# First pass of three projections: a tile's products moved from four turns behind to one, first weights in four parts, loads reordered

## The chip, the cores and the metric

The kernel runs on one core of a Trainium2 chip. The metric is the device time of one execution in microseconds (us); the kernel before takes 2210.08 us, the median of three runs (2209.09 to 2212.71). The profile comes from one more execution, of 2207.55 us, whose span of profiled work is 2205.8 us.

Names of engines: PE is TensorE with its matmuls, PEld its loading of the stationary operand, DVE is VectorE, ACT is ScalarE, POOL is GpSimd. SPq is the queue of SyncE, from which most DMAs are issued; ACTq are the DMAs that ScalarE issues.

## The reference

One inference step of a two-layer decoder, float32 throughout, for 1024 prompt rows and 32 sample rows that share the weights (D_MODEL is 1024):

```
layer 0: h0 = rmsnorm(x) @ even_w_in          # 1024 x 3584
         mix0 = dilated attention, retention  # of h0
         x1 = x + (mix0 * silu(gate columns of h0)) @ even_w_out    # 1024 x 1024
layer 1: h1 = rmsnorm(x1) @ odd_w_in          # 1024 x 2864
         mix1 = sparse attention              # of h1
         x2 = x1 + (mix1 * silu(gate columns of h1)) @ odd_w_out    # 1024 x 1024
         y = rmsnorm(x2)
```

The attention parts are not touched by the change. It concerns the three places where rows are multiplied with a weight matrix.

## The kernel before

The program is a row of phases, each with its own buffers and semaphores and a barrier of all engines at its end. In a phase every engine has its own list of instructions, in an order written out by hand, and each instruction starts when those ahead of it on its engine have started and the semaphores that it names have come. `project` is the first phase of work (h0). `project_out` is called twice: in the middle, for x1 and then, with no barrier between, h1 (called projection 2 here), and at the end of the program, for x2 and y (projection 3). `project` is projection 1. All three begin in the same way, and only this beginning, the first pass, is changed.

The rows are cut into nine tiles: eight of 128 prompt rows (t = 0 to 7) and one of the 32 sample rows (t = 8). The columns of the weights are cut into passes (seven of 512 columns in projection 1; three of 342, 342 and 340 in projection 3 and at the start of projection 2). In the first pass a tile goes through these steps:

- SPq loads it, 512 KB, into one of two buffers `x`. In projections 2 and 3 two gate loads of together another 512 KB go to a buffer `z` (line 680 and 683; in projection 2 both buffers lie in `cmp_w1`, which the trace shortens to `cmp_w`; in projection 3 the gate is one DMA). From t = 2 on the load waits until tile t - 2 has been turned.
- ACT takes the sum of squares and its root (L352, L355), or the SiLU of the gate (L806); DVE scales the rows (L419, L421) or multiplies them with the gate (L896).
- PE turns the tile: eight transposes by a product with the identity matrix into one of two PSUM buffers `tps` (L518, L1034).
- ACT copies it out rounded, as `y_hi` (L360, L827), and DVE writes what was lost by the rounding, `y_lo` (L427, L910).
- PE makes the 24 matmuls of a tile's product (L527, L1047): for each of 8 blocks k of 128 rows of the weights, y_lo with w_hi, y_hi with w_lo, y_hi with w_hi. DVE takes the product out of PSUM (`take_product`, L445, L939) and SPq stores it.

The weights of a pass are cut in the same way into `w_hi` (ACT, L366, L833) and `w_lo` (DVE, L436, L922), from one buffer `w_raw` that one DMA fills: 2048 KB in projection 1, 1368 KB in the others. Weights of the passes lie in turns in two halves of w_hi and w_lo.

The constant LAG = 4 sets the order on PE: tiles 0 to 4 are turned, then PE waits for the whole of the first weights (`w_cut`), then come the product of tile 0, the turn of tile 5, the product of tile 1, and so on. WEIGHT_AT = 2 puts the cutting of the first weights on ACT and DVE behind their work on tile 2. Their load is issued by ACT once the rows of tile 0 have landed. The loads of the weights of the second pass, of the gain `g` (first in projection 1) and of the two first pieces of `w_side` (weights for the sample rows) stand behind the loads of all nine tiles on SPq, and the stores of the first pass behind those.

Ahead of projection 1 is a phase of its own in which SPq loads the identity matrix (`constants_shared`, 64 KB) and waits for it.

```
543                for t, n in tiles:
544                    turn(t, n)
545                    if t == LAG:
546                        pe.wait_ge(w_cut, 1)
547                    if t >= LAG:
548                        pe.wait_ge(yT_written[(t - LAG) % 2], (t - LAG) // 2 + 1)
549                        products(0, t - LAG)
```

## Time and profile before

| | |
|---|---|
| median of three runs | 2210.08 us (2209.09 to 2212.71) |
| the profiled execution | 2207.55 us |
| its span | 2205.8 us, 34764 instructions |
| PE busy | 1964.5 us (89%) |
| DVE, ACT, POOL busy | 849.7, 703.7, 508.4 us |
| DMA | 261.54 MB, mean 119 GB/s |

Each row of a timeline gives the start in us, how long it took, the engine, the line of the kernel, the operation with output and input, how many were merged, and in brackets how long the engine had been idle before it and what ended that. A busy PE is the sum of its matmuls' times; they overlap, and their distance is less than their length. The idle PE of the program's first 40 us, and of the same stage of the two other projections, is what the following reads.

### The profile page before, as it was taken

What the parts mean: (1) busy time and instruction counts of PE and PEld (TensorE: products, weight loads), DVE (VectorE), ACT (ScalarE), POOL (GpSimd) and SP (SyncE); (2) the same over time, 40 slices, a digit from 0 to 9 for tenths busy, and PEclk for the clock granted to TensorE, in tenths of its full rate; (3) what the DMA queues carried; (4) which work ended last, traced back from release to release, by engine and by line L of the source; (5) the groups of instructions that cost most, each with busy time, mean ns of one, the idle gap of its engine ahead of it and who ended that gap; (6) DMA issues with size and microseconds to landing.
All of it is one profiled execution on the core that took longest, in us unless ns stands there. A gap on an engine that the chain in (4) does not pass through costs nothing. (4 is left out here: it accounts for less than half of the span.)

```text
span 2205.8 us, 34764 instructions
## 1 busy us (share of the span) xinstructions
PE 1964.5 (89%) x13406; PEld 1444.6 (65%) x13406; DVE 849.7 (39%) x2373; ACT 703.7 (32%) x1555; POOL 508.4 (23%) x621
## 2 busy tenths in 40 slices
PE   4999998997883998999969999994999999999596
PEld 4777775565661987788855555553666666666495
DVE  4212212564442334122312112123666666666433
ACT  4100001553322222010012232323656666566312
POOL 0000000876640000000031211101454444445000
PEclk9999999999995999999989999997999999999798
DMA  3444434545595753744182323106000000000565
GB/s 131 175 142 142 141 131 124 176 118 152 163 242 165 239 189 108 241 154 147 48 242 96 135 74 135 49 1 162 7 21 21 16 21 21 6 11 11 194 214 182
DMA packets 163025, 261.54 MB, mean 119 GB/s; under 512 B 33746, under 2 KB 113296, under 8 KB 158512
## 3 DMA queue, kind: packets, MB, share of 16 engines
q1 hardware_dynamic: 141712, 207.83, 29.7%
q0 software_dynamic: 4608, 33.56, 4.2%
q10 hardware_dynamic: 16544, 17.95, 2.9%
q8 instruction: 109, 1.79, 0.3%
q14 instruction: 52, 0.43, 0.1%
HBM read 210.57 MB, written 55.77 MB: 121 GB/s over the span
## 5 line engine op out<-in xcount | busy, mean ns | idle before, releaser
L1573 POOL TENSOR_SCALAR sparse_pr<-sparse_pr,sparse_coef,sparse_gate 128x63 f32<-128x63 f32 (+8 forms) x384 | 247.4, 663 | 324.6 <-DVE sparse_coef L1537 324.6
L1047 PE MATMUL x_acc<-x_w_hi,x_y_lo 128*128 128x478 f32 (+3 forms) x768 | 274.7, 358 | 0.0
L1047 PE MATMUL x_acc<-x_w_lo,x_y_hi 128*128 128x478 f32 (+3 forms) x768 | 269.5, 351 | 0.0
L1047 PE MATMUL x_acc<-x_w_hi,x_y_hi 128*128 128x478 f32 (+3 forms) x768 | 269.1, 350 | 0.0
L2606 PE MATMUL ss_ps_h<-ss_xT,cmp_w 128*128 128x508 f32 x512 | 244.0, 594 | 0.8 <-ACT ss_xT L2445 0.8
L1475 ACT ACTIVATE sparse_pr<-sparse_pr,sparse_nmax 128x63 f32<-128x63 f32 (+8 forms) x384 | 227.8, 599 | 3.9 <-DVE sparse_nmax L1530 3.9
L1575 POOL TENSOR_SCALAR dilated_pr<-dilated_pr,dilated_coef 128x1024 f32<-128x1024 f32 (+7 forms) x64 | 109.5, 1725 | 408.1 <-DVE dilated_coef L1537 408.1
L1404 PE MATMUL sparse_ps_t<-constants_shared,sparse_pr 128*128 128x128 f32 (+1 forms) x1184 | 170.2, 281 | 11.3 <-ACT sparse_prT L1298 6.3
L527 PE MATMUL h_acc<-h_w_hi,h_y_lo 128*128 128x512 f32 x448 | 177.6, 397 | 0.0
L1530 DVE CUSTOM_DVE_ANT_0 sparse_pr<-sparse_ps_s,constants_sparse 128x63 f32<-128x63 f32 (+4 forms) x384 | 144.5, 421 | 85.4 <-PE sparse_ps_s L1392 85.3
L527 PE MATMUL h_acc<-h_w_hi,h_y_hi 128*128 128x512 f32 x448 | 175.2, 391 | 0.0
L527 PE MATMUL h_acc<-h_w_lo,h_y_hi 128*128 128x512 f32 x448 | 175.1, 391 | 0.0
L1404 PEld LDWEIGHTS sparse_ps_t<-constants_shared,sparse_pr 128*128 128x128 f32 (+1 forms) x1184 | 126.0, 140 | 74.5 <-issue 50.5
L1047 PEld LDWEIGHTS x_acc<-x_w_hi,x_y_lo 128*128 128x128 f32 x768 | 146.4, 191 | 25.1 <-issue 14.7
L1392 PE MATMUL sparse_ps_s<-sparse_kT_all,sparse_qT 64*128 64x512 f32 (+3 forms) x800 | 154.5, 484 | 2.7 <-ACT sparse_kT_all L1298 1.3
L1047 PEld LDWEIGHTS x_acc<-x_w_lo,x_y_hi 128*128 128x128 f32 x768 | 146.4, 191 | 10.2
L1047 PEld LDWEIGHTS x_acc<-x_w_hi,x_y_hi 128*128 128x128 f32 x768 | 146.0, 190 | 10.8
L1431 PE MATMUL sparse_ps_o<-sparse_prT,sparse_v_all 128*64 128x128 f32 x2112 | 148.9, 280 | 0.0
L1298 ACT COPY sparse_prT<-sparse_ps_t 128x512 f32<-128x512 f32 (+3 forms) x176 | 90.3, 513 | 175.7 <-PE sparse_ps_t L1404 175.5
L445 DVE COPY h_out<-h_acc 128x512 f32<-128x512 f32 x56 | 38.7, 692 | 248.9 <-PE h_acc L527 244.4
L1431 PEld LDWEIGHTS sparse_ps_o<-sparse_prT,sparse_v_all 128*64 128x64 f32 x2112 | 112.2, 136 | 25.7 <-issue 25.7
L2606 PEld LDWEIGHTS ss_ps_h<-ss_xT,cmp_w 128*128 128x128 f32 x512 | 86.1, 190 | 54.9 <-issue 53.6
(345 smaller groups left out, 2761.8 us busy)
## 6 DMA issues: line engine op xcount, KB each, us to landing
h_w_side<-in_even_w_in SPq DMA_DIRECT2D x16, 896.0 KB, 5.0
h<-h_out SPq DMA_DIRECT2D x56, 256.0 KB, 2.0
h_w_raw<-in_even_w_in SPq DMA_DIRECT2D x6, 2048.0 KB, 8.0
x_w_side<-in_odd_w_in SPq DMA_DIRECT2D x16, 716.0 KB, 4.8
x_w_raw<-in_odd_w_in SPq DMA_DIRECT2D x5, 1912.0 KB, 8.7
h<-x_out SPq DMA_DIRECT2D x40, 239.0 KB, 2.2
ev_unit<-in_cache_a_k SPq DMA_DIRECT2D x4, 2048.0 KB, 9.6
ev_unit<-in_cache_a_v SPq DMA_DIRECT2D x4, 2048.0 KB, 11.1
```

Of the source, the lines that this page charges most:

```text
L445: nc.vector.tensor_copy(outb[:, b, 0:width(i)], acc[b][:, 0:width(i)]).then_inc(evacuated[b], 1)
L527: last = nc.tensor.matmul(acc[b][:, 0:width(i)], rows[:, k, t * P:(t + 1) * P], buffer_of(cols, i)[:, k, :], start=(k == 0 and a == 0), st ...
L1047: last = nc.tensor.matmul(acc[b][:, 0:passes[p][3]], left[:, k, t * P:(t + 1) * P], weights(right, p)[:, k, :], start=(k == 0 and a == 0), ...
L1298: ins = nc.scalar.copy(to, src) if scale is None else nc.scalar.activation(to, src, ACT.Copy, scale=scale)
L1392: ins = nc.tensor.matmul(ps_s[c % 2][e][:, a - c0:b - c0], qT[i % 2][half, t * P:(t + 1) * P], rhs, start=True, stop=True)
L1404: last = nc.tensor.transpose(to[0:w, c - c0:c - c0 + P], pr[u % UB][:, e, c:c + w], con("ident"))
L1431: ins = nc.tensor.matmul(out, lhs, rhs, start=k == first and x == 0 and c == a, stop=k == end - 1 and last_one)
L1475: nc.scalar.activation(row, row, ACT.Exp, scale=-1.0, bias=nmax[u % UB][:, e * NBR + br:e * NBR + br + 1], accum_out=lsum[u % UB][:, e * N ...
L1530: nc.vector.tensor_tensor_reduce(out=pr[u % UB][:, e, a:b], in0=ps_s[c % 2][e][:, a - c0:b - c0], in1=bias, scale=1.0, scalar=so_far, op0= ...
L1573: nc.gpsimd.tensor_scalar(row, row, one, gate[:, t, 2 * i + e, (br + 1) % 3:(br + 1) % 3 + 1], ALU.mult, ALU.mult).then_inc(scaled, 1)
L1575: nc.gpsimd.tensor_scalar(row, row, one, None, ALU.mult).then_inc(scaled, 1)
L2606: ins = nc.tensor.matmul(ps_h[c][:, 0:4 * NCS], comp.w1[m][:, l, c * P:(c + 1) * P], xT[m][:, :, l % KD, s:s + NCS], start=l == 0, stop=l ...
```

## The change

In all three projections:

- PE: tile 0 and tile 1 are turned, then comes the product of tile 0, then the turn of tile 2, the product of tile 1, and so on: the product of tile t follows the turn of tile t + 1. LAG and WEIGHT_AT are gone.
- The first weights are loaded, rounded and cut in four parts of two blocks k each, with a semaphore for each load and one that counts the parts that are cut (`first_cut`). PE waits for part k // 2 at blocks k = 0, 2, 4, 6 of the first product.
- SPq issues: rows of tile 0 (in projection 1 then the identity and `g`), weight part 0, rows of tile 1, parts 1 to 3, rows of tile 2. From there on each tile's load is followed by a store of the product three tiles back, and the load of the second pass's weights stands behind the rows of tile 4. `g` (projections 2 and 3) and `w_side` come behind the rows of the last tile.
- ACT and DVE: parts 0 and 1 are cut around their work on tile 1, parts 2 and 3 behind the copy of tile 0. DVE takes the product of tile t - 2 in its step on tile t. The second pass's weights are rounded on ACT in its step on tile 6, and cut on DVE behind the product of tile 5, in its step on tile 7. The residual of tile t is loaded by ACT in its step on tile t.

In projection 1 alone: the phase for the identity matrix is gone, and its load is one of the phase; the mean with its epsilon, made by a small DVE instruction (L417) between the square and the root, is now the scale and bias of the root. Branches of `project` that no call used are deleted.

```diff
-LAG = 4
-WEIGHT_AT = 2
+FIRST_PARTS = 4
@@ project, SPq
-                for t, n in tiles:
...
-                for i in range(n_chunks):
-                    if i + 1 < n_chunks:
-                        sp.wait_ge(w_cut, i + 1)
-                        load_w(sp, i + 1)
-                    if i == 0:
-                        for s in range(WS):
-                            load_side(s)
+                load_rows(0, P)
+                constants.load(sp, ident_in)
+                sp.dma_start(g[:, :], gain.partition_broadcast(P)).then_inc(gain_in, 16)
+                load_first(0)
+                load_rows(1, P)
+                for j in range(1, FIRST_PARTS):
+                    load_first(j)
+                for t, n in tiles[2:]:
+                    load_rows(t, n)
+                    if t == 4:
+                        load_w(1)
+                    if t >= 3:
+                        store(0, t - 3)
+                for s in range(WS):
+                    load_side(s)
+                for t in range(NT - 2, NT):
+                    store(0, t)
@@ project, ACT
-                act.wait_ge(loaded[0], 16 * n_loads)
-                load_w(act, 0)
+                act.wait_ge(eps_ready, 1)
+                stats(0, P)
+                first_high_part(0)
+                stats(1, P)
+                first_high_part(1)
+                evacuate(0)
+                for j in range(2, FIRST_PARTS):
+                    first_high_part(j)
+                for t, n in tiles[2:]:
                     stats(t, n)
-                    if t:
-                        evacuate(t - 1)
-                    if t == WEIGHT_AT:
-                        w_high_part(0)
+                    evacuate(t - 1)
+                    if t == CUT_AFTER + 1:
                         w_high_part(1)
@@ project, DVE (project_out alike)
+                rows_of(0, P)
+                first_low_part(0)
+                rows_of(1, P)
+                first_low_part(1)
+                y_low_part(0)
+                for j in range(2, FIRST_PARTS):
+                    first_low_part(j)
+                for t, n in tiles[2:]:
                     rows_of(t, n)
-                    if t:
-                        y_low_part(t - 1)
-                    if t == WEIGHT_AT:
-                        w_low_part(0)
-                    if t > LAG:
-                        take_product(0, t - LAG - 1)
+                    y_low_part(t - 1)
+                    take_product(0, t - 2)
+                    if t - 2 == CUT_AFTER:
+                        w_low_part(1)
@@ project, PE (project_out alike)
                     for k in range(KD):
+                        if i == 0 and t == 0 and k % KP == 0:
+                            pe.wait_ge(first_cut, k // KP + 1)
...
+                turn(0, P)
+                for t, n in tiles[1:]:
                     turn(t, n)
-                    if t == LAG:
-                        pe.wait_ge(w_cut, 1)
-                    if t >= LAG:
-                        pe.wait_ge(yT_written[(t - LAG) % 2], (t - LAG) // 2 + 1)
-                        products(0, t - LAG)
+                    pe.wait_ge(yT_written[(t - 1) % 2], (t - 1) // 2 + 1)
+                    products(0, t - 1)
@@ project_out, SPq
+                load_gated(0, P)
+                load_first(sp, 0)
+                load_gated(1, P)
+                for j in range(1, FIRST_PARTS):
+                    load_first(sp, j)
+                for t, n in tiles[2:]:
                     load_gated(t, n)
+                    if t == 4:
+                        load_w(sp, 1)
+                    if t >= 3:
+                        store(0, t - 3)
@@ build
-        with Phase(nc) as phase, nc.Block() as block:
-            constants_in = phase.semaphore("constants_in")
...
```

Three places of the instruction order show it. The first is the start of SPq's list, in projection 1. Before:

```order
L2922 DMA constants_shared<-in_const 128x128
L159 ISA
L284 UNCONDITIONAL_BRANCH
L287 DMA h0_g<-in_even_norm 128x1024
L296 DMA h0_x<-in_x_prompt 128x1024 x8
L296 DMA h0_x<-in_x_sample 32x1024
L281 DMA h0_w_raw<-in_even_w_in 128x8x512
```

and now:

```order
L250 DMA h0_x<-in_x_prompt 128x1024
L2858 DMA constants_shared<-in_const 128x128
L282 DMA h0_g<-in_even_norm 128x1024
L254 DMA h0_w_raw<-in_even_w_in 128x2x512
L250 DMA h0_x<-in_x_prompt 128x1024
L254 DMA h0_w_raw<-in_even_w_in 128x2x512 x3
L250 DMA h0_x<-in_x_prompt 128x1024 x2
L272 DMA h0<-h0_out 128x512
L250 DMA h0_x<-in_x_prompt 128x1024
L261 DMA h0_w_raw<-in_even_w_in 128x8x512
L272 DMA h0<-h0_out 128x512
L250 DMA h0_x<-in_x_prompt 128x1024
```

What moved: the rows of tile 0 go first and the weights stand second, fourth and fifth instead of on ACT behind the landing of tile 0 (where they were `h0_w_raw`, 128x8x512); a store of `h0_out` and the second pass's weights (128x8x512) stand between loads of rows.

The second is the start of PE's list, in projection 1, with the waits. tps0 and tps1 hold turned tiles, acc0 a product. Before:

```order
L518 MATMUL h0_tps0<-constants_shared,h0_x 128x128 [waits h0_rows_ready0]
L518 MATMUL h0_tps0<-constants_shared,h0_x 128x128 x7
L518 MATMUL h0_tps1<-constants_shared,h0_x 128x128 [waits h0_rows_ready1]
L518 MATMUL h0_tps1<-constants_shared,h0_x 128x128 x7
L518 MATMUL h0_tps0<-constants_shared,h0_x 128x128 [waits h0_yT_written0,h0_rows_ready0]
L518 MATMUL h0_tps0<-constants_shared,h0_x 128x128 x7
L518 MATMUL h0_tps1<-constants_shared,h0_x 128x128 [waits h0_yT_written1,h0_rows_ready1]
L518 MATMUL h0_tps1<-constants_shared,h0_x 128x128 x7
L518 MATMUL h0_tps0<-constants_shared,h0_x 128x128 [waits h0_yT_written0,h0_rows_ready0]
L518 MATMUL h0_tps0<-constants_shared,h0_x 128x128 x7
L527 MATMUL h0_acc0<-h0_w_hi,h0_y_lo 128x512 [waits h0_yT_written0,h0_w_cut]
L527 MATMUL h0_acc0<-h0_w_lo,h0_y_hi 128x512
```

and now:

```order
L431 MATMUL h0_tps0<-constants_shared,h0_x 128x128 [waits h0_rows_ready0,h0_ident_in]
L431 MATMUL h0_tps0<-constants_shared,h0_x 128x128 x7
L431 MATMUL h0_tps1<-constants_shared,h0_x 128x128 [waits h0_rows_ready1]
L431 MATMUL h0_tps1<-constants_shared,h0_x 128x128 x7
L442 MATMUL h0_acc0<-h0_w_hi,h0_y_lo 128x512 [waits h0_first_cut,h0_yT_written0]
L442 MATMUL h0_acc0<-h0_w_lo,h0_y_hi 128x512
...
L442 MATMUL h0_acc0<-h0_w_hi,h0_y_lo 128x512 [waits h0_first_cut]
...
L431 MATMUL h0_tps0<-constants_shared,h0_x 128x128 [waits h0_yT_written0,h0_rows_ready0]
L431 MATMUL h0_tps0<-constants_shared,h0_x 128x128 x7
L442 MATMUL h0_acc1<-h0_w_hi,h0_y_lo 128x512 [waits h0_yT_written1]
```

What moved: the first product comes after two turns instead of five, and it waits for `first_cut`, part by part, instead of for `w_cut`; each later tile's turn stands between two products.

The third is DVE's list in projection 2: `cmp_w1_1` is the gating of a tile's rows, `x1_y_lo` the cutting of a turned tile, `x1_w_lo` that of weights, `x1_out` the taking of a product. Before:

```order
L896 TENSOR_TENSOR cmp_w1_1<-cmp_w1_1 128x1024 x2
L910 TENSOR_TENSOR x1_y_lo<-x1_tps0,x1_y_hi 128x8x128
L896 TENSOR_TENSOR cmp_w1_1<-cmp_w1_1 128x1024
L910 TENSOR_TENSOR x1_y_lo<-x1_tps1,x1_y_hi 128x8x128
L922 TENSOR_TENSOR x1_w_lo<-x1_w_raw,x1_w_hi 128x8x342
L896 TENSOR_TENSOR cmp_w1_1<-cmp_w1_1 128x1024
L910 TENSOR_TENSOR x1_y_lo<-x1_tps0,x1_y_hi 128x8x128
L896 TENSOR_TENSOR cmp_w1_1<-cmp_w1_1 128x1024
L910 TENSOR_TENSOR x1_y_lo<-x1_tps1,x1_y_hi 128x8x128
L896 TENSOR_TENSOR cmp_w1_1<-cmp_w1_1 128x1024
L910 TENSOR_TENSOR x1_y_lo<-x1_tps0,x1_y_hi 128x8x128
L939 TENSOR_TENSOR x1_out<-x1_acc0,x1_res 128x342
```

and now:

```order
L828 TENSOR_TENSOR cmp_w1_1<-cmp_w1_1 128x1024
L854 TENSOR_TENSOR x1_w_lo<-x1_w_raw,x1_w_hi 128x2x342
L828 TENSOR_TENSOR cmp_w1_1<-cmp_w1_1 128x1024
L854 TENSOR_TENSOR x1_w_lo<-x1_w_raw,x1_w_hi 128x2x342
L842 TENSOR_TENSOR x1_y_lo<-x1_tps0,x1_y_hi 128x8x128
L854 TENSOR_TENSOR x1_w_lo<-x1_w_raw,x1_w_hi 128x2x342 x2
L828 TENSOR_TENSOR cmp_w1_1<-cmp_w1_1 128x1024
L842 TENSOR_TENSOR x1_y_lo<-x1_tps1,x1_y_hi 128x8x128
L876 TENSOR_TENSOR x1_out<-x1_acc0,x1_res 128x342
L828 TENSOR_TENSOR cmp_w1_1<-cmp_w1_1 128x1024
L842 TENSOR_TENSOR x1_y_lo<-x1_tps0,x1_y_hi 128x8x128
L876 TENSOR_TENSOR x1_out<-x1_acc1,x1_res 128x342
```

What moved: the cut of tile t - 1 stands behind the gating of tile t as before, but the product of tile t - 1 now needs it at once, where there were three tiles of turned rows in stock.

## Rows read from the trace of the kernel before

**Rows 1.** Waits of PE, one query for each projection's stage: total us, times, longest

```profile
PE h_tps L518 <- DVE h_x L421: 28.0, 4, 15.0
...
PE x_tps L1034 <- DVE cmp_w L896: 37.7, 5, 25.5
...
PE x_tps L1034 <- DVE x_x L896: 24.9, 4, 13.4
```

**Rows 2.** Timeline of the program's start, projection 1

```profile
0.73 0.38 SPq L2922 DMA_DIRECT2D constants_shared<-in_const  x1
...
9.50 1.28 ACT L352 ACT_TABLE_LOAD   x1 [9.50 <-DMA h_x<-in_x_prompt]
...
13.70 1.28 DVE L421 SCALAR_TENSOR_TENSOR h_x<-h_x,h_stat,h_g 128x1024 f32<-128x1024 f32 x1
...
15.04 3.79 PE L518 MATMUL h_tps<-constants_shared,h_x 128*128 128x128 f32 x16 [15.04 <-DVE h_x L421]
...
22.84 3.61 ACT L366 CAST h_w_hi<-h_w_raw 128x4096 fp32r<-128x4096 f32 x1
...
26.49 4.43 DVE L436 TENSOR_TENSOR h_w_lo<-h_w_raw,h_w_hi 128x4096 fp32r<-128x4096 f32 x1 [1.78 <-ACT h_w_hi L366]
```

**Rows 3.** Timeline of PE in projection 1: turns and first matmul

```profile
35.73 1.97 PE L518 MATMUL h_tps<-constants_shared,h_x 128*128 128x128 f32 x8 [0.98 <-DVE h_x L421]
...
37.35 0.78 PE L527 MATMUL h_acc<-h_w_hi,h_y_lo 128*128 128x512 f32 x1
...
44.92 1.04 PE L518 MATMUL h_tps<-constants_shared,h_x 128*128 128x128 f32 x8
...
51.26 1.04 PE L518 MATMUL h_tps<-constants_shared,h_x 128*128 128x128 f32 x8
```

**Rows 4.** Timeline of projection 2's first pass

```profile
695.66 2.36 DVE L896 TENSOR_TENSOR cmp_w<-cmp_w 128x1024 f32<-128x1024 f32 x2 [7.99 <-ACT cmp_w L806]
...
696.94 3.64 PE L1034 MATMUL x_tps<-constants_shared,cmp_w 128*128 128x128 f32 x16 [25.53 <-DVE cmp_w L896]
...
698.94 0.32 SPq L680 DMA_DIRECT2D cmp_w<-mix  x1
...
699.99 1.23 DVE L910 TENSOR_TENSOR x_y_lo<-x_tps,x_y_hi 128x1024 fp32r<-128x1024 f32 x1 [1.97 <-ACT x_y_hi L827]
...
704.34 1.06 ACT L806 ACTIVATE cmp_w<-cmp_w 128x1024 f32<-128x1024 f32 x1 [4.38 <-DMA cmp_w<-h]
...
717.22 0.63 PE L1047 MATMUL x_acc<-x_w_hi,x_y_lo 128*128 128x342 f32 x1
...
722.96 1.09 PE L1034 MATMUL x_tps<-constants_shared,cmp_w 128*128 128x128 f32 x8
...
724.08 0.32 SPq L680 DMA_DIRECT2D cmp_w<-mix  x1
...
727.63 1.03 PE L1034 MATMUL x_tps<-constants_shared,cmp_w 128*128 128x128 f32 x8
...
731.11 1.06 ACT L806 ACTIVATE cmp_w<-cmp_w 128x1024 f32<-128x1024 f32 x1 [5.92 <-DMA cmp_w<-h]
...
733.49 1.09 PE L1034 MATMUL x_tps<-constants_shared,cmp_w 128*128 128x128 f32 x8 [1.07 <-DVE cmp_w L896]
```

**Rows 5.** Stretches of projection 2: start:end and length, busy us by engine, PEclk, DMA share, GB/s

```profile
701.00:703.00 2.00, 0.00 (x0) 0.00 (x0) 0.22 (x1) 0.00 (x0) 0.00 (x0) 1.00 0.98 346
...
705.00:707.00 2.00, 0.29 (x2) 0.29 (x3) 1.57 (x2) 2.00 (x3) 0.00 (x0) 0.50 0.44 167
```

**Rows 6.** DMA issues of projection 1's stage: size, median us to landing

```profile
h_x<-in_x_prompt SPq DMA_DIRECT2D x8, 512.0 KB, 3.8
...
h_w_raw<-in_even_w_in ACTq DMA_DIRECT2D x1, 2048.0 KB, 7.8
```

**Rows 7.** Timeline of PE in projection 3: first turn, first matmul

```profile
2062.69 3.43 PE L1034 MATMUL x_tps<-constants_shared,x_x 128*128 128x128 f32 x16 [13.43 <-DVE x_x L896]
...
2083.15 0.64 PE L1047 MATMUL x_acc<-x_w_hi,x_y_lo 128*128 128x342 f32 x1
```

More of the change, by code:

```diff
@@ L395, in _ @@
-                if residual is not None:
-                    load_side_residual(0)
-                for i in range(1, n_chunks):
-                    for t in range(NT):
-                        if residual is not None:
-                            load_residual(i, t)
-                        if t == CUT_AFTER and i + 1 < n_chunks:
-                            w_high_part(i + 1)
+                    nc.scalar.copy(weights(w_hi, i), w_raw[:, :, 0:width(i)]).then_inc(w_high, 1)
+                act.wait_ge(eps_ready, 1)
```

337 lines of the change are left out of this document (123 added, 214 removed).

## The prediction

> **What bounds the kernel now.** The page gives PE 1964.5 us of the 2205.8 us span, so what a stage is worth is PE's idle time in it. I read the waits of PE first. In the three stages PE waits almost only to turn rows: 28.0 us in projection 1, 37.7 in projection 2 (25.5 of it ahead of the first turn), 24.9 in projection 3 (13.4 ahead of the first turn) [rows 1]. Then the timelines, to see what those waits end in. In projection 1 the first turn is at 15.04 and the first product at 37.35 [rows 2, 3]; in projection 2 they are at 696.94 and 717.22, in projection 3 at 2062.69 and 2083.15 [rows 4, 7]. These 20 to 22 us hold five turns and nothing else for PE; from the first product on it hardly stops (one more wait of 1.07 us in projection 2 [rows 4]). So the term to work out is when the first product can start, and what comes back later in the pass.
>
> **Projection 1, the start.** The identity load at 0.73 and its phase go; the rows of tile 0 are issued at that time instead. A 512 KB load of rows takes a median 3.8 us to land [rows 6]: 4.6. Before, ACT began at 9.50 and DVE could scale at 13.70 [rows 2], 4.2 us for table loads, square and root; the small DVE step that leaves lay beside the second table load, so I count nothing for it. Scaling is at 8.8, and 1.3 later, at 10.1, PE turns tile 0 at the low clock, 2.0 us (35.73 shows one at that pace [rows 3]), to 12.1. ACT rounds part 0 (a quarter of 3.61, 0.9), takes tile 1's root, rounds part 1: done by 12. Then its copy of tile 0, 1.0, ends at 13.1. DVE: part 0 (a quarter of 4.43, 1.1) to 11.2, tile 1's scaling 1.5 to 12.7, part 1 to 13.8, y_lo of tile 0 (1.2) to 15.0. I add 0.3, since tile 1's rows are behind `g` and part 0 in the queue. **The first product starts at 15.3, not 37.35: 22.0 us earlier.** Parts 2 and 3 are cut at 16.1 and 17.2; the product reaches them after 12 and 18 of its 24 matmuls, 2.7 and 4.0 us on at the high clock. The cover of part 3 is thus 2 us; 3.7 MB are ahead of its landing, which at the 300 to 350 GB/s of a loaded stretch [rows 5] is 11 to 12 us, at about 14.
>
> What comes back: turns 2, 3 and 4 now stand between products, at about 1.04 each [rows 3]: -3.1. Tile 0's product took 44.92 - 37.35 = 7.57 us, a later tile with its turn 51.26 - 44.92 = 6.34, the product alone then 5.4 [rows 3]: the low clock cost 2.1. Now PE is busy from 10.1 almost without a gap, and I count half of this back, +1.0. At the pass's end DVE cuts the second weights (4.43) between the product of tile 5 and the scaling of tile 8; the scaling is then 6.8 us behind the start of turn 7, and PE wants it at 6.4: with y_lo of tile 7 behind it -0.7. Row loads have slack: 6.4 us per tile for 512 KB. **Sum: 22.0 - 3.1 + 1.0 - 0.7 = 19.2 us.**
>
> **Projection 2, the start.** Up to the first turn at 696.94 nothing changes. ACT: SiLU of tile 0, done when the gating starts at 695.66 [rows 4], part 0 (342 of 512 columns, so 0.6), SiLU of tile 1 when its rows are in. Ahead of these now lie 2.45 MB instead of 2.1; at about 340 GB/s that is 1.1 us more, 696.7. Then part 1, and the copy of tile 0 behind its turn at 698.9, to 699.95. DVE: gating of tile 1 to 699.0, part 1 (0.75) to 699.8, y_lo 699.95 to 701.2. First product: **701.3, not 717.22: 15.9 us earlier.** From the turns to the product no gap is left. After those two turns the granted clock went to 1.00 (2.4 GHz) at 701, with PE idle, and was back at 0.50 (1.2 GHz) at 705 [rows 5]; the new product begins inside that stretch, so the low clock's price in the first product (722.96 - 717.22 = 5.74 against 4.67 - 1.0 = 3.7 [rows 4], less what is idle: 1.7) comes back. Turns 2 to 4: -3.1. The idle 1.1 before goes into the new sum of stalls.
>
> The stalls are the dear unknown. A tile's rows are 1 MB, its load waits for the turn two tiles back, and behind its landing come SiLU 1.06, gating 1.23, turn 1.0 [rows 4]. Landing took from 698.94 to 704.34, 5.4 us, beside the weights, and at worst from 724.08 to 731.11, 7.0 us [rows 4]. PE needs 4.67 per tile [rows 4], so two tiles give 9.3 us; less the last three items 6.0 are left for a load. Worked through: turn 2 can start at 706.6, while product 0 ends at 705.05 (-1.5, and 0.25 for y_lo of tile 1). Loads 3 and 4 fit. The second weights, 1368 KB or 4.1 us of the queue at 340 GB/s, are ahead of load 5, which lands near 720.8: -2.2. Loads 6 and 7 fit. The cut of the second weights (4.43 x 342/512 = 3.0) ahead of gating tile 8: -0.5. Together 4.5. Bounds: 0 each if every load lands in under 6.0, 9 to 10 if all land in 7.0 (two tiles then take 10.3, 0.5 more per tile or 3.5 in all), the second weights cost their 4.1 in full and turn 2 its 1.5; I take 4.5, nearer the 5.4 row. **Sum: 15.9 - 3.1 + 1.7 + 1.1 - 4.5 = 11.1 us.**
>
> **Projection 3** is the same chain with the first turn at 2062.69: first product at 2067.1 instead of 2083.15 [rows 7], 16.0. Turns -3.1, the clock +1.4 (it was low for 3.0 us), no wait of before to give back, stalls -4.5: **9.9 us** (16.0 - 3.1 + 1.4 - 4.5 = 9.8, rounded up for one gate DMA less).
>
> **Costed at nothing:** earlier stores and later `g` and `w_side` (wanted only in the second pass, some 13 us behind their issue; if that cover goes, 1 or 2 us); SPq's wait for a product's copy ahead of the next load (this ends about when the turn does that the load waits for anyway); the dead branches.
>
> Total 19.2 + 11.1 + 9.9 = 40.2 us, of 2207.55 in the profiled execution. That one lies 2.5 us under the median of the runs, so from 2210.08: **2169.9, I say 2170 us**. No part behind the three passes is shared with them; what PE gains there nothing else holds up.
>
> **A rule against the change.** The trace has 512 KB in 3.8 us and 2048 KB in 7.8 [rows 6]: if parts of 512 KB each took their 3.8 in turn, the last would land 7.4 us later. But rows, gain and weights in one queue overlap, and the stage reaches 346 GB/s [rows 5], so I take the queue as one stream. The Trainium skill (DMA: Bandwidth & Descriptors, Bandwidth) says to batch DMAs to at least 1 MiB for 75% of peak. The trace agrees for one DMA alone, not for a queue of them; by that rule this is rival A.
>
> **Rivals.**
> - A, late loads: the parts and the rows land one after another. For it: the 7.0 us landing, and a DMA share of 0.98 in projection 2 [rows 4, 5]. Against: PE hardly waited in the old pass, at the same pace of loads. Part 3 would come 7.4 us later with a cover of 2 and 1, so 4 to 5 us in projection 1, and the full stalls (10 instead of 4.5) in the two others: 40 - 5 - 11 = 24, so 2186 us.
> - B, less stall: every load lands in under 6.0 and the clock is up from the first matmul on. 1 + 3.5 + 3.5 more: 2162 us.
> - C, slower than before: the clock. With row loads gating every tile, PE may stand between products long enough for the clock to fall, and then stay at 1.2 GHz for the pass. For it: PE is at 0.50 at 705 in projection 2, where it waits 37.7 - 25.5 = 12.2 us in four turns [rows 1, 5]. Against: turns behind the wait of 1.07 still take 1.09, the high clock [rows 4]. A turn takes 1.97 at the low clock and 1.04 at the high one [rows 3]; a product at the same ratio 7.0 instead of 3.7. That is 4.2 more per tile, 34 per projection: 2210 - 40 + 68 = 2238 us. It decides for slower from about 10 low tiles of 16 on, where 40 / 4.2 is reached, and needs waits of several us at every tile. The Trainium skill (TensorE: Matmul & The Clock Gate, Loop structure matters more than you think) names a DMA wait ahead of the matmuls as what makes them run at the low clock; here no wait that long is expected.
> - D, no gain: the early start only moves the wait, to the start of the second pass, if its weights are cut no earlier than before (DVE has them at about 736 in my chain, the pass begins at 743). It would need 7 us and more of delay in all three: 2208 us.
>
> **Chances.** Forecast 0.65 (its own range 2163 to 2178), A 0.19, B 0.08, C 0.05, D 0.03. A difference under about 0.2%, 4.4 us, can't be told from none here. Faster 0.92, same 0.03, slower 0.05. The range, 2158 to 2188, takes in B and A with their bounds and leaves out C and D.
>
> **What the new profile would show.** First matmul of the products near 15.3, about 4.4 us behind the first turn in projections 2 and 3, with the high clock within the first product. PE waits in the first pass of about 1, 4 and 4 us, the longest ahead of turn 5 for the loads behind the second weights. Second passes 19, 11 and 10 us nearer to their first turns or the start. Wrong would be: a first product that waits at block 4 or 6 for `first_cut`, waits ahead of every turn, or a product of 7 us in the middle of a pass of projection 2 or 3.

## The result, and the profile after

The changed kernel takes **2175.76 us** (median of 4 runs, 2174.89 to 2176.33) against 2209.59 us beside it (2206.5 to 2212.71): ratio 0.9846, 95% interval 0.9831 to 0.9861, so 33.8 us less. A second session gave 2176.61 against 2208.36, ratio 0.9857 (0.9842 to 0.9872). The forecast was 2170, range 2158 to 2188: the time is inside it, and the gain smaller than forecast. The profiled execution took 2175.72 us, span 2173.9, so 31.9 of the forecast's 40.2 us are seen in the spans.

The waits of PE after, by stage (total us, times, longest); they answer to [rows 1]:

```profile
PE h_tps L431 <- DVE h_x L361: 10.9, 3, 10.1
PE h_acc L442 <- DVE h_y_lo L367: 0.8, 2, 0.5
...
PE x_tps L973 <- DVE cmp_w L828: 29.4, 3, 23.7
PE x_tps L973 <- DVE cmp_w L835: 3.2, 1, 3.2
PE x_acc L988 <- DVE x_y_lo L842: 0.5, 1, 0.5
...
PE x_tps L973 <- DVE x_x L828: 17.9, 3, 13.4
```

Projection 1 has lost all waits but the one ahead of its first turn and 1.6 us in four small ones. Projections 2 and 3 keep that too, and two more: 2.6 and 2.0 us ahead of turn 1, and 3.2 and 2.5 us ahead of turn 5. (Line 828 is the gating. Line 835 is another operation, the scaling of x1's rows for h1; its wait, ahead of a turn at 777.78, lies behind the first pass.)

Projection 1's start after, from the timeline (start, duration, instruction, [idle before it <- releaser]), to be laid beside [rows 2, 3]:

```profile
4.29 1.28 ACT L319 ACT_TABLE_LOAD   x1 [4.29 <-DMA h_x<-in_x_prompt]
...
8.65 1.28 DVE L361 SCALAR_TENSOR_TENSOR h_x<-h_x,h_stat,h_g 128x1024 f32<-128x1024 f32 x1
...
10.08 1.94 PE L431 MATMUL h_tps<-constants_shared,h_x 128*128 128x128 f32 x8 [10.08 <-DVE h_x L361]
...
14.92 0.79 PE L442 MATMUL h_acc<-h_w_hi,h_y_lo 128*128 128x512 f32 x1 [0.30 <-DVE h_y_lo L367]
...
22.22 1.04 PE L431 MATMUL h_tps<-constants_shared,h_x 128*128 128x128 f32 x8
```

The chain runs as worked out: table load, scaling at 8.65 (8.8 was forecast), turn at 10.08 (10.1), first product at 14.92 (15.3; 37.35 before).

Projection 2's first pass after, to be laid beside [rows 4]:

```profile
670.71 1.28 ACT L732 ACT_TABLE_LOAD   x1 [32.73 <-PEq L159]
...
678.83 1.97 PE L973 MATMUL x_tps<-constants_shared,cmp_w 128*128 128x128 f32 x8 [23.70 <-DVE cmp_w L828]
680.98 1.06 ACT L732 ACTIVATE cmp_w<-cmp_w 128x1024 f32<-128x1024 f32 x1 [1.90 <-DMA cmp_w<-h]
683.35 1.97 PE L973 MATMUL x_tps<-constants_shared,cmp_w 128*128 128x128 f32 x8 [2.55 <-DVE cmp_w L828]
685.26 0.65 PE L988 MATMUL x_acc<-x_w_hi,x_y_lo 128*128 128x342 f32 x1
...
692.73 0.43 SPq L585 DMA_DIRECT2D x_w_raw<-in_even_w_out  x1
...
695.89 0.54 SPq L597 DMA_DIRECT2D cmp_w<-mix  x1
...
705.65 1.06 ACT L732 ACTIVATE cmp_w<-cmp_w 128x1024 f32<-128x1024 f32 x1 [6.37 <-DMA cmp_w<-h]
...
708.01 1.94 PE L973 MATMUL x_tps<-constants_shared,cmp_w 128*128 128x128 f32 x8 [3.17 <-DVE cmp_w L828]
...
714.31 0.93 PE L973 MATMUL x_tps<-constants_shared,cmp_w 128*128 128x128 f32 x7
```

The second weights (1368 KB) are issued at 692.73, tile 5's rows behind them at 695.89. They are there only when SiLU starts at 705.65, and PE has waited 3.17 us. Then comes what no step of the forecast had: turn 5 takes 1.94 us, the pace of the low clock, where turns 2 to 4 take 1.04 to 1.09. The next turn follows after 6.3 us, not 4.6. (A turn's distance to the next is taken from start to start.)

For this and the other kernels I use three durations from each profile: P1, from the start of the span to VectorE's taking of tile 7's product in projection 1's first pass; P2 and P3, from VectorE's first instruction in projections 2 and 3 to the same point there. The last columns are the median and its ratio to the kernel before in the same session. Names are explained with the experiments.

```
                    P1     P2     P3    median   ratio (95% interval)
before            86.78  67.13  64.71  2209.59
before, again     85.66  66.83  64.81  (one run, 2206.85)
after             67.54  58.17  57.37  2175.76  0.9846 (0.9831-0.9861)
after, again      66.69  58.27  58.22  2176.61  0.9857 (0.9842-0.9872)
p1_only           66.44  66.63  66.15  2190.02  0.9910 (0.9896-0.9924)
one_part          75.11  63.01  63.15  2191.68  0.9915 (0.9901-0.9929)
lag2              98.38  82.38  76.22  2246.99  1.0156 (1.0137-1.0176)
late_w            66.42  56.32  54.81  2173.31  0.9840 (0.9826-0.9854)
warm              66.05  57.70  57.88  2174.31  0.9842 (0.9825-0.9859)
quick             67.42  56.22  55.34  2167.88  0.9816 (0.9802-0.9829)
quick_late        68.86  55.00  57.79  2170.47  0.9837 (0.9820-0.9854)
quick_warm        65.91  55.41  52.37  2168.80  0.9799 (0.9785-0.9812)
spread            67.72  55.47  52.34  2165.22  0.9786 (0.9773-0.9799)
spread_warm       65.94  52.48  50.56  2163.55  0.9783 (0.9770-0.9797)
```

### The profile page after: what moved, and what is told of

Its sections match the earlier page's. It is cut to its first block and busy times, and to the rows that moved or that the text cites. A ratio compares the mean times of both kernels' runs of the same rounds, so it can differ in the third digit from the quotient of the medians.

```text
span 2173.9 us, 34766 instructions
## 1 busy us (share of the span) xinstructions
PE 1963.1 (90%) x13406; PEld 1442.1 (66%) x13406; DVE 848.3 (39%) x2374; ACT 704.9 (32%) x1564; POOL 506.3 (23%) x621
## 5 line engine op out<-in xcount | busy, mean ns | idle before, releaser
L988 PEld LDWEIGHTS x_acc<-x_w_hi,x_y_lo 128*128 128x128 f32 x768 | 146.7, 191 | 27.4 <-issue 14.6
```

The source lines that it names most:

```text
L988: last = nc.tensor.matmul(acc[b][:, 0:passes[p][3]], left[:, k, t * P:(t + 1) * P], weights(right, p)[:, k, :], start=(k == 0 and a == 0), ...
```

## Experiments

### Are the three projections independent, and is the rest of the program touched?

**before_again** is the kernel before and **after_again** the changed one, both unedited. **p1_only** has the changed `project` and the `project_out` of before.

> The kernel before, profiled a second time. Between the end of projection 1's first pass and the start of projection 2 the five profiles with the new projection 1 lost 2.1 to 3.0 us against the one profile of before. Theory A (scatter: that one profile, at 2207.55 against a median of 2209.3, was quick there): here the stretch from the last product of projection 1 to projection 2's first instruction takes 323 to 325 us instead of 321.6. Theory B (a cost of the change in code that it doesn't touch): 321.6 within 0.5.

> The kernel after the change, timed in the same session as the two below. 2173 to 2177. The two waits of about 3 us ahead of turn 5 in projections 2 and 3 stand there again, with the low clock behind them, if they are properties of the program: 2.5 to 3.5 us and 2.0 to 3.0 us. That the first product of projection 1 starts at 15.2 and the pass ends 19 to 20.5 us earlier than before's repeats too.

> Projection 1 as after the change, projections 2 and 3 as before it. Theory (each projection pays for itself, nothing behind it is shared): the 19.2 us that the profile after shows at the last product of projection 1 stay, so the median stands 16 to 19 us below before's, 2191 to 2194. Rival (the two later projections pay only because they start in another state of queues and clock, or the first one's gain is eaten behind it): a gain under 14 us. It also tells whether the 3.0 us lost between projection 1 and projection 2 belong to the change: if they do, projection 2's first load stands 16.2 us earlier than before's here too; if they are scatter between executions, somewhere between 16 and 20.

Measured: p1_only is 19.3 us below before, just outside the 16 to 19 expected; its P2 is before's within 0.5 us and its P3 1.4 longer. The rival (under 14) falls. From projection 1's last product to projection 2's first instruction the profile of before took 321.6 us, before_again 323.6, after 324.6, after_again 323.8 and p1_only 324.1; over all profiles taken it is 321.4 to 324.8, with nothing in common among the short ones. So this is scatter, and before's profiled execution was at the quick end. From projection 2's tile 7 to projection 3 it is 1299.0 to 1302.4 us, and here scatter may not be all: the three profiles with the `project_out` of before have 1299.0 to 1299.7, ten of the eleven with the new one 1300.2 to 1302.4 (the last is quick, 1299.3). Some 1.5 us of the gain may be lost there; the rows do not say by what, and no run tested it. The three passes alone gain 34.8 us by the means of both pairs of profiles (19.1, 8.8 and 7.0). The spans show 31.9 and 32.0, the medians 33.8 and 31.8.

The wait ahead of turn 5 repeats, 3.34 and 3.10 us, and so does the low clock behind it (expected were 2.5 to 3.5 and 2.0 to 3.0, so the second is just above). Projections 2 and 3 after, again, from the timeline of PE:

```profile
706.56 1.76 PE L973 MATMUL x_tps<-constants_shared,cmp_w 128*128 128x128 f32 x7 [3.34 <-DVE cmp_w L828]
...
2065.00 1.33 PE L973 MATMUL x_tps<-constants_shared,x_x 128*128 128x128 f32 x5 [3.10 <-DVE x_x L828]
```

(The rows end within the turns: 7 turns of 1.76 and 5 of 1.33 are 0.25 us each, against 0.13 at the high clock.)

### What are the four parts worth?

```diff
-FIRST_PARTS = 4
+FIRST_PARTS = 1
-load_first(0); load rows of tile 1; load_first(1 to 3)
+load rows of tile 1; load_first(0)
-first_high_part(0); tile 1; first_high_part(1); evacuate(0); ...
+tile 1; evacuate(0); first_high_part(0)      (VectorE likewise)
```

> After's order of turns and products, but the first weights as one load of 2048 KB behind tile 1's rows, cut in one piece (hi about 3 us on ScalarE, lo about 3.4 us on VectorE) behind tile 0's evacuation. Theory A (the parts matter where products begin with the weights, and the passes are paced by PE once they have begun): the first product begins 7 to 8 us later in projection 1 and 5 to 7 us later in projections 2 and 3; of that the stall ahead of turn 5 gives back 2 to 3 us in each of the latter, so the sum is 11 to 17 us slower than the full change, 2187 to 2193. Theory B (rows, not weights, limit: the passes are bound by their loads): projection 1 loses its 7 but projections 2 and 3 end where they do now, 2181 to 2184. If the parts were worth nothing and the order alone paid, 2176.

Measured: 2191.68, theory A's range. P1 is 7.6 to 8.4 us longer than in the two profiles after, P2 4.8, P3 4.9 to 5.8: 18 in all, 16 in the medians. The price is one row in each projection, the wait for the whole cut; here projection 2, timeline of PE:

```profile
688.95 1.97 PE L957 MATMUL x_tps<-constants_shared,cmp_w 128*128 128x128 f32 x8 [1.24 <-DVE cmp_w L815]
695.95 0.62 PE L972 MATMUL x_acc<-x_w_hi,x_y_lo 128*128 128x342 f32 x1 [5.03 <-DVE x_w_lo L841]
```

So about half of the change's gain is the parts'. The other half is what one_part keeps: the order of turns and products, the order of the loads and, in projection 1, the phase of the identity matrix that is gone. The phase that is gone can be up to 5 of projection 1's remaining 11 us, since the first turn is at 10.18 in one_part and at 15.04 before; these three were not run apart. I had expected 2 to 3 us back ahead of turn 5 in projections 2 and 3. Nothing came back: the waits there are 3.36 and 2.84 us. Behind the first of them the clock did not fall; this turn took 1.09 us and the next followed after 4.99:

```profile
720.39 1.09 PE L957 MATMUL x_tps<-constants_shared,cmp_w 128*128 128x128 f32 x8 [3.36 <-DVE cmp_w L815]
```

### Products one turn further behind

```diff
-turn(0); for t = 1..8: turn(t); products(0, t - 1)
+turn(0); turn(1); for t = 2..8: turn(t); products(0, t - 2)
+products(0, 7)
```

> The full change, but the products of a tile follow the turn two tiles on (turns 0, 1, 2, then the products of tile 0), in all three projections. Projection 1: VectorE has tile 2's rows ready at 18.5, so the first product starts at 19.5 to 20 instead of 15.2; turn 2 (1 to 2 us) is then already done, so the first pass ends 3 to 4 us later. Projections 2 and 3: tile 2's rows can only be loaded when turn 0 has freed its buffer, so turn 2 comes at about 18 us after the phase's first instruction and the first product 3 to 4 us later than now. Theory A (what is lost ahead of the first product is lost at the end of the pass): 8 to 11 us slower than the full change, 2184 to 2187. Theory B (in projections 2 and 3 the stall ahead of turn 5 takes it back, since tile 5's rows land when they land): 3 to 5 us slower in all, 2179 to 2181.

Measured: 2246.99, some 70 us slower than the change (66 to 69 by the ratios) and slower than before. Both theories are wrong by far. I had moved PE's order and left VectorE's, which still takes product t-2 ahead of the scaling of tile t+1. On PE that product now ends directly ahead of turn t+1, so turns 3 to 7 each wait for a copy and a scaling. Projection 1, the waits of PE, then timelines of VectorE and of PE:

```profile
PE h_tps L431 <- DVE h_x L361: 32.3, 9, 10.3
```

```profile
26.99 0.69 DVE L389 COPY h_out<-h_acc 128x512 f32<-128x512 f32 x1 [7.06 <-PE h_acc L442]
27.60 0.15 DVE L359 RECIPROCAL h_stat<-h_stat 128x1 f32<-128x1 f32 x1
27.79 1.28 DVE L361 SCALAR_TENSOR_TENSOR h_x<-h_x,h_stat,h_g 128x1024 f32<-128x1024 f32 x1
```

```profile
29.13 1.97 PE L431 MATMUL h_tps<-constants_shared,h_x 128*128 128x128 f32 x8 [2.17 <-DVE h_x L361]
...
39.38 1.97 PE L431 MATMUL h_tps<-constants_shared,h_x 128*128 128x128 f32 x8 [2.18 <-DVE h_x L361]
...
49.66 1.10 PE L431 MATMUL h_tps<-constants_shared,h_x 128*128 128x128 f32 x8 [2.17 <-DVE h_x L361]
```

0.69, 0.15 and 1.28 make up 2.12 of the 2.17 of the wait. In most tiles the clock falls as well: three of the four distances between turns 3 and 7 are 10.25 to 10.35 us instead of 6.34, and the one in which it stays high is 8.74. This is the prediction's rival C: a wait at every tile, with turns at the low clock. It had 2238 us; here it is 2247, and it came from the order of VectorE, not from loads. The run shows what a lag costs if only PE's order is moved; it doesn't price a later first product, for which VectorE's order would have to move too. That was not tried.

### What makes the wait ahead of turn 5, and what does the clock cost?

**late_w** loads projection 2's and 3's second weights behind the last tile's rows; **warm** fills PE's waits with transposes.

```diff
-if t == 4: load_w(sp, 1)
+if t == 8: load_w(sp, 1)
-w_high_part(1), w_low_part(1) behind tile 5
+w_high_part(1), w_low_part(1) at the end of the first pass
```

```diff
+for _ in range(48): nc.tensor.transpose(acc_s[:, 0:P], ident, ident)
 turn(0, P, False)
+for _ in range(18): ...                    (projection 1: 30 and 8)
```

> The full change, but in projections 2 and 3 the second pass's weights (2048 KB) are loaded behind the last tile's rows instead of ahead of tile 5's, and cut at the end of the first pass. Theory A (the wait of 3.17 and 2.46 us ahead of turn 5 is tile 5's rows queued behind these weights, and the low clock behind it is its consequence): both waits go, the next turn follows 4.7 and not 6.3 us later, and each first pass ends 4 to 5 us earlier; the weights land some 8 us before the second pass starts or, if late, cost up to 2 us of it. Sum 6 to 10 us faster than the full change: 2166 to 2170. Rival B (the loads are bound by bandwidth in all, and the rows of tiles 5 to 8 just meet the same bytes, or the cut now stands ahead of the second pass): the wait moves to the start of the second pass and the sum is within 2 us of the full change, 2174 to 2178.

> The full change with transposes of the identity into a bank that nothing reads before its own start (30 ahead of the first turn and 8 behind it in projection 1, 48 and 18 in projections 2 and 3), in time in which PE waits. They change no output. Theory A (the low clock at the start of the first pass costs what the rows at either level say: turn 1.97 instead of 1.0, and some 14 matmuls at 0.29 instead of 0.16 us): the first turns take 1.0 us, the first product starts about 1 us earlier, its matmuls run at the high clock, and each projection ends 1.5 to 3 us earlier unless the weights' parts or rows then arrive too late; sum 3 to 8 us faster, 2168 to 2173. Rival B (the first product then only waits for the cut of the parts, and in projections 2 and 3 for tile 5's rows behind the second weights): projections 2 and 3 gain nothing, projection 1 1 to 2 us, sum 2174 to 2176. If the dummies outlast the wait, their surplus delays the first turn and shows in it as a busy PE ahead.

late_w: the expectation's 2048 KB should read 1368 KB. The wait of 3 us is gone, as theory A has it, and no turn between 2 and 8 shows the low clock. But P2 and P3 lose only 1.9 and 3.0 us against the mean of the two profiles after (and that in the fastest of the five executions). The median, 2173.31, is in neither theory's range, and it can't tell the kernels apart (the intervals overlap). From turn 4 to turn 7 the turns stand 5.0 to 5.8 us apart. Projection 2, timelines of PE and of ACT:

```profile
697.74 1.04 PE L971 MATMUL x_tps<-constants_shared,cmp_w 128*128 128x128 f32 x8
...
703.15 1.09 PE L971 MATMUL x_tps<-constants_shared,cmp_w 128*128 128x128 f32 x8 [0.32 <-DVE cmp_w L827]
...
708.36 1.09 PE L971 MATMUL x_tps<-constants_shared,cmp_w 128*128 128x128 f32 x8
...
714.14 1.09 PE L971 MATMUL x_tps<-constants_shared,cmp_w 128*128 128x128 f32 x8 [0.64 <-DVE cmp_w L827]
```

```profile
705.99 1.06 ACT L732 ACTIVATE cmp_w<-cmp_w 128x1024 f32<-128x1024 f32 x1 [3.25 <-DMA cmp_w<-h]
```

From the turn at 697.74 to the one two tiles on, at 708.36, are 10.6 us: the turn frees the buffer, the rows are issued behind a store and have landed when SiLU starts at 705.99, then come SiLU, gating and turn. PE alone would take 2 x 4.62. So the weights make most of the wait, as theory A had it, and the round trip over two row buffers stands right behind, which it had not. (The idle ahead of a turn is shown too small in such rows, since the ends of matmuls are modelled; the distances of the starts are not.)

warm: the transposes do their work. Projection 2's turns 0 and 1 take 1.09, and the products start at the high clock. Yet P2 and P3 are within 0.6 us of the change. Turn 5 waits all the same, 2.04 us, and the clock falls behind it. PE in projection 2, timeline, then stretches (PEclk is the third figure from the end, ahead of the DMA share and GB/s):

```profile
677.33 1.09 PE L977 MATMUL x_tps<-constants_shared,cmp_w 128*128 128x128 f32 x8 [1.80 <-DVE cmp_w L832]
...
704.55 1.09 PE L977 MATMUL x_tps<-constants_shared,cmp_w 128*128 128x128 f32 x8 [2.04 <-DVE cmp_w L832]
...
711.07 1.04 PE L977 MATMUL x_tps<-constants_shared,cmp_w 128*128 128x128 f32 x8
```

```profile
705.00:707.00 2.00, 1.96 (x11) 1.72 (x10) 1.16 (x3) 1.20 (x2) 0.00 (x0) 0.66 0.19 66
707.00:709.00 2.00, 2.00 (x9) 2.00 (x9) 2.00 (x2) 2.00 (x2) 0.00 (x0) 0.50 0.79 221
709.00:711.00 2.00, 2.00 (x14) 2.00 (x14) 0.25 (x1) 1.14 (x1) 0.00 (x0) 0.98 0.95 308
```

Rival B holds by its time and by the wait that stays: with rows as the bound, the clock at the start cost nothing that these runs can see in projections 2 and 3. In projection 1, where nothing waits later, the three profiles with these transposes have P1 65.9 to 66.1, the seven without them (same code there) 66.4 to 68.9.

### Shorter ways for rows and second weights

**quick** shortens the round trip; **quick_late** has the second weights behind tile 7's rows; **quick_warm** adds the transposes to quick; **spread** loads the second weights in four parts; **spread_warm** has both.

```diff
 def load_gated(t, n):
-    wait turned[b]; rows; gates         (one semaphore)
+    wait rows_ready[b]; gates           (z_in[b], SiLU waits for this)
+    wait turned[b]; rows                (loaded[b])
-store(0, t - 3) behind the loads of t
+store(0, t - 4)
```

```diff
-if t == 4: load_w(sp, 1)
+if 4 <= t < NT: load_second(sp, t - 4)   (342 KB each; cut whole, at the end)
```

> The full change, with three edits to the rows' way in projections 2 and 3: a tile's gates are loaded ahead of its rows, on a semaphore of their own, so that SiLU runs beside the landing of the rows; the gates of tile t are loaded when VectorE has multiplied tile t-2, not when PE has turned it; a tile's store is issued behind the next tile's load. The second weights stay ahead of tile 5's rows. Theory A (after the stall of the weights has been taken away, what remains is the round trip over two row buffers: turn, load, SiLU, multiply, 10.6 us for two tiles against 9.35 that PE takes): the first turn comes about 1 us earlier, the wait ahead of turn 5 shrinks from about 3 to 1 to 2 us and with it the low clock goes; 2 to 3 us in each projection, sum 4 to 6 us faster than the full change. Rival B (the bytes in flight are the bound, each load just lands later): within 1.5 us of the full change.

> The same with the second weights of projections 2 and 3 (1368 KB) behind tile 7's rows and cut at the end of the first pass. Theory A: no wait over 0.5 us ahead of any turn but the first two, turns 4.7 to 4.9 us apart up to turn 7, so that each first pass ends some 2 us earlier than with the late weights alone and 5 to 6 us earlier than in the full change; sum 9 to 12 us faster than the full change, 2164 to 2167. Rival B (bandwidth): the turns stay 5.2 to 5.8 us apart as with the late weights alone, sum 2170 to 2173. Rival C (the cut at the end of the pass holds the second pass up by 1 to 3 us in each projection): the passes end early, but the second begins late; 2168 to 2171.

> The quicker way of the rows (gates first, on their own semaphore) with the transposes of the identity in PE's waits ahead of the first products; they change no output. Without the quicker rows these transposes gained under 1 us, with the first products at the high clock and the wait ahead of turn 5 as it was. In the profile of the quicker rows the low clock covers the first two turns (1.97 instead of 1.05 us) and 20 products of tile 0 (0.285 instead of 0.157 us apart). Theory A (the low clock now stands on the path): turn 2 follows turn 1 after 6 to 6.5 us instead of 8.8, each projection ends 2 to 3.5 us earlier, sum 4 to 7 us faster than without the transposes, 2161 to 2164. Theory B (tile 5's rows behind the second weights decide anyway, and its wait just grows from 2 to 4 us, with the low clock behind it): within 1.5 us of it, 2167 to 2169.

> The quicker way of the rows, with the second weights of projections 2 and 3 loaded in four parts of 342 KB, one behind each of tiles 4 to 7, and cut in one piece at the end of the first pass. Theory A (a whole load of 1368 KB stalls whichever rows stand behind it, tile 5's when it is early, tile 8's when it is late, and each stall of over 1.5 us brings the low clock; a part of 342 KB fits into a tile's slack of 4.6 us): all turns from 2 to 8 stand 4.6 to 5.0 us apart, no wait over 0.5 us, and each projection ends 1.5 to 3 us earlier than with the quicker rows alone; sum 3 to 5 us faster, 2163 to 2165. Rival B (1.7 MB for each tile in 4.62 us, 370 GB/s, is what the queues can do at best): turns 5 to 8 stand 5.0 to 5.6 us apart, no gain, 2167 to 2169. Rival C: the cut at the end delays the second pass by 1 to 2 us; 2166 to 2167.

> The spread second weights and the transposes of the identity in PE's waits together (no output changes). If rows, weights and clock are the three things left in the starts of projections 2 and 3, their gains add up here: all turns 4.6 to 5.0 us apart from turn 2 on, turn 2 at 6 to 6.5 us behind turn 1, 2157 to 2161, below both kernels by 49 and 16 us. If the earlier products only bring PE to rows that are not there, turns 3 to 8 show waits of 0.3 to 1 us each and the time stays at that of the spread weights alone, 2163 to 2165.

quick: 2167.88 against 2176.61 of the change in the same session, and the intervals don't overlap: 8.7 us, more than theory A's 4 to 6. P2 and P3 are 2.0 and 2.5 us shorter than in the profiles after, within its 2 to 3; where the rest comes from the profiles do not show. The wait ahead of turn 5 is 1.67 and 1.27 us, as theory A has it, with the clock at 2.4 GHz behind it. The bytes are the same, so the way of the rows held the turns up, at least in part. Which of its three changes (gates first on their own semaphore, gates loaded earlier, store later) did it was not run apart.

quick_late: turns 2 to 7 stand 4.62 us apart to the hundredth in projection 2, so the round trip is gone. Theory A's time is not reached all the same, 2170.47. The weights now stand ahead of tile 8's rows, and turn 8 waits instead of turn 5 (0.95 us in projection 2). The time is also in the ranges of rivals B and C, but not their mechanisms: the turns are not 5.2 us apart, and from tile 7 of projection 3 to the end of the program it takes 86.4 us, quick 86.9, so the late cut holds nothing up there. Projection 3, timeline of PE, then stretches:

```profile
2067.75 1.03 PE L974 MATMUL x_tps<-constants_shared,x_x 128*128 128x128 f32 x8
...
2074.17 0.83 PE L974 MATMUL x_tps<-constants_shared,x_x 32*128 32x32 f32 x8 [1.58 <-DVE x_x L830]
```

```profile
2076.00:2078.00 2.00, 2.00 (x8) 2.00 (x8) 1.83 (x1) 0.14 (x1) 0.00 (x0) 0.50 0.60 192
2078.00:2080.00 2.00, 2.00 (x8) 2.00 (x8) 1.18 (x1) 0.00 (x0) 0.00 (x0) 0.50 0.02 6
```

A wait of 1.58 us, and PE is at 0.50 for nearly the whole product behind it, until 2081.2: P3 is 2.4 us longer than quick's.

spread: 2165.22, and PE waits nowhere in projection 3 from turn 2 on, with turns 4.65 apart. In projection 2, turns 6 and 7 came 5.0 and 5.6 us behind the ones before. Here the queues are full. Stretches of projection 2:

```profile
698.00:702.00 4.00, 4.00 (x30) 3.98 (x29) 1.32 (x2) 1.90 (x2) 0.00 (x0) 1.00 1.02 372
702.00:706.00 4.00, 4.00 (x30) 3.98 (x29) 1.97 (x3) 1.63 (x2) 0.00 (x0) 1.00 1.02 335
```

Rival B's limit is thus close (projection 3 has the same DMA share, 1.00 to 1.04, and no wait). The whole load was the trouble at both places that were tried with the quicker rows: theory A holds in projection 3 and half in projection 2. Its threshold does not: waits of 1.59 us (warm, turn 4 of projection 3) and more left the clock high. The third place, behind the last tile's rows as in late_w, was not tried with the quicker rows. Spread's ratio to before is 0.9786, quick's 0.9816, from two sessions, with intervals that miss each other by 0.0003 only. spread_warm: 2163.55, **the fastest: 48 us below before** (45 to 51 by its ratio's interval), and 14 to 16 below the change by the difference of the ratios. Its turns in projection 2:

```profile
693.52 1.04 PE L984 MATMUL x_tps<-constants_shared,cmp_w 128*128 128x128 f32 x8
...
702.77 1.03 PE L984 MATMUL x_tps<-constants_shared,cmp_w 128*128 128x128 f32 x8
...
712.10 1.09 PE L984 MATMUL x_tps<-constants_shared,cmp_w 128*128 128x128 f32 x8
```

The transposes shorten P2 and P3 by 3.0 and 1.8 us against spread, and by 0.8 and 3.0 against quick; the medians (2163.55 against 2165.22 in one session) and the ratios (0.9799 and 0.9816, overlapping) can't tell that from none, and quick_warm's 2168.80 is not the 2161 to 2164 of its theory A but in theory B's range; nor is spread_warm in its 2157 to 2161. What they bring when rows are there stays open. In quick_warm the wait ahead of turn 5 grew to 2.6 us in projection 2, not to 4, and the clock did not fall behind it. Timeline of PE:

```profile
704.34 1.09 PE L980 MATMUL x_tps<-constants_shared,cmp_w 128*128 128x128 f32 x8 [2.61 <-DVE cmp_w L835]
```

## Why the prediction was right, and where it was off

- **Projection 1**: forecast 19.2; 19.2 in the first pair of profiles, 19.0 in the second. First product 22.4 us earlier (22.0). From it to tile 7 the pass takes 3.2 us more, 3.6 in the second pair (forecast: 3.1 for turns, less 1.0 of clock, plus 0.7 of cut, 2.8). The terms are less good than their sum: the first product with turn 2's start took 7.3 us against 7.57 before, so the clock gave back 0.3 (nothing in the second pair), and the cut delayed turn 8 by 0.3; two errors of opposite sign.
- **Projection 2, the start**: the first product comes 15.7 us earlier within its stage (15.2 in the second pair), about as forecast (15.9), but two steps on the way were wrong and cancelled. I wrote that up to the first turn nothing changes. It came 9.9 us into the stage in both profiles of before, and comes 8.1 and 9.2 into it in the two after. What has changed ahead of it is ACT's table load of 1.28 us, which stood behind the landing of tile 0 (below, before) and now stands at the stage's first moment, 670.71. That this is the cause was not tested apart. And the first product is 6.4 us behind the first turn, not 4.4: tile 1's rows land late, SiLU starts 2.2 us behind the turn and not ahead of it, and PE waits 2.55 us.

```profile
693.27 1.28 ACT L806 ACT_TABLE_LOAD   x1 [39.01 <-DMA cmp_w<-h]
```

- **Projection 3, the start**: 14.6 us earlier (14.9 in the second pair), not 16.0, by the same late rows of tile 1, with nothing to cancel them: the first turn stands where it stood in its stage, though the table load has moved there too.
- **The stalls** are the term that was mis-sized most. I had 4.5 in each. Taking 4.62 as a tile, the distances of the turns in projection 2 after (6.82, 4.61, 4.91, 8.32, 6.30, 4.61, 4.85 from turn 1 on) hold, from turn 2 on, 3.7 at turn 5, 1.7 in the tile behind it and 0.5 elsewhere: 5.9. Projection 3 holds 5.0 in the same way. That the longest wait of the pass would stand ahead of turn 5, for rows behind the second weights, was right. The wait at turn 2 that I expected (1.75) wasn't there, the one at turn 5 was larger than 2.2, and the low clock behind it was in no term: I had argued from the wait of 1.07 us [rows 4] that PE keeps its clock, and a wait of 3 us is another case. late_w shows the main cause of the wait; warm, that the fall can come behind it also when the clock was high from the start (in quick_warm and in projection 2 of one_part it did not come).
- **The clock at the start**: I had the high clock within the first product and 1.7 us back from it. The first product with turn 2's start took 4.9 us against 5.7 before: 0.8 back. In projection 3 it is 0.8 too, where I had 1.4.
- **Sum**: P2 9.0 and 8.6 (forecast 11.1), P3 7.3 and 6.6 (9.9). With P1's 19.1 that is 34.8, as said above, against 40.2. That nothing behind the passes is shared is not refuted, but not shown either: the gain of projection 1 came through whole in p1_only, while behind projection 2's first pass some 1.5 us may be lost (above). The result lies inside the range; that errors of opposite sign cancelled in projection 1 and at the start of projection 2 was luck.
- **Rivals**: A's queue of parts one after another did not come in projection 1, where PE never waits for a part; the rows behind the second weights were late, as its second half says. (The 346 GB/s that I set against A is a stretch of 2 us in projection 2 [rows 5]; I had no such row for projection 1.) C did not come here, but lag2 shows that its mechanism exists and what it costs. The Trainium skill (DMA: Bandwidth & Descriptors, Bandwidth) has the rule to batch DMAs to at least 1 MiB. Here four parts (512 KB in projection 1, 342 KB in the others) beside rows kept the first products fed, and spread, with 342 KB parts for the second weights too, was faster than one load of 1368 KB. So for a queue that carries rows on a deadline these runs speak against following it. They do not measure the rate of small parts against that of large ones.

## What to carry to other kernels

Start the products as soon as the first operands are there, and cut the first load so that they are; then look at who stands behind each large load in the queue, because it stalls whatever has a deadline there, and try it in parts that fit the slack of one tile. When an order is moved on one engine, walk through the order of the engines that feed it: a lag that fits one order can cost a wait at each tile in another.

## What the runs showed of the hardware

- How long PE waits doesn't decide alone whether its clock falls. Behind waits of 3.17 and 2.46 (after), 2.04 (warm) and 1.58 us (quick_late, projection 3) the matmuls ran at 1.2 GHz. Behind 0.64 (late_w), 1.07 us [rows 4], 1.67 (quick), 2.61 (quick_warm) and 3.36 (one_part, projection 2) they stayed at 2.4. From the turn behind a long wait to the next one took 5.0 us where the clock stayed (quick, quick_warm, one_part) and 6.1 to 6.5 where it fell (after, after_again, warm): the fall cost 1.1 to 1.5 us. In quick_late, where the clock stayed low for the whole product, it was more: from turn 8 to the taking of tile 7's product 7.9 us against quick's 5.2.
- A short pause went with a clock that stayed low: in after, after_again and late_w no pause stands between turn 1 and the first product of projections 2 and 3, and turn 2 follows after 6.3 to 6.8 us; in quick, quick_late and spread VectorE's y_lo leaves a pause of 0.6 us there, and turn 2 follows after 8.4 to 9.2 us, in quick's projection 2 with matmuls 0.285 us apart from 684.3 to 689.5. That the pause is the cause was not tested apart.
- A DMA of 1368 KB cost the most where a deadline stood behind it: with it as one load ahead of their rows turn 5 or turn 8 waited 0.9 to 3.4 us; in four parts behind four tiles (spread) the waits from turn 2 on are 0.5 us at most, and with it behind the last rows (late_w) 0.7 us.
